# DeltaNet heads: turning the triangular inverses on VectorE, and one run of weight products per level

## The reference

```
# per head, direction and chunk of 64 tokens (the kernel takes blocks of 128)
L = jnp.where(strict, jnp.einsum('bhncd,bhnjd->bhncj', kb, k) * decay, 0.0)
A = L + jnp.eye(C, dtype=L.dtype)
rhs = jnp.concatenate([vb, kb * jnp.exp(gc)[..., None]], axis=-1)
sol = lax.linalg.triangular_solve(A, rhs, left_side=True, lower=True, unit_diagonal=True)
u, w = sol[..., :dv], sol[..., dv:]
...
s = jnp.einsum('bhgqd,bhkd->bhgqk', q_blk, k) * scale
p = jax.nn.softmax(s, axis=-1)
o = jnp.einsum('bhgqk,bhkd->bhgqd', p, v)
```

## Time and profile before

| | us |
|---|---|
| median of 3 runs | 2656.44 (2653.32 to 2656.96) |
| profiled execution, its own time | 2658.15 |
| its span, first to last instruction | 2656.5 |
| TensorE busy | 2560.8, 96% |
| VectorE busy | 1425.2, 54% |
| ScalarE busy | 1022.2, 38% |
| GpSimd busy | 214.3, 8% |
| turns of T (L1669), busy, 448 instructions | 58.0 |
| mean granted clock of TensorE | 0.983 |

### The profile page before, as it was taken

How to read it: one execution, slowest core, us unless ns; L and a number is a source line. 1 busy time by engine, 2 the same in 40 slices (tenths; PEclk the granted TensorE clock), 3 DMA queues, 4 the chain that set the end, 5 groups by cost and what they waited for, 6 DMA issues and landing times.

```text
span 2656.5 us, 35703 instructions
## 1 busy us (share of the span) xinstructions
PE 2560.8 (96%) x12302; PEld 2098.3 (79%) x12302; DVE 1425.2 (54%) x1854; ACT 1022.2 (38%) x1428; POOL 214.3 (8%) x286
## 2 busy tenths in 40 slices
PE   4999999999999899979999999999999999999997
PEld 4777788888887688857888888888888888888885
DVE  6736666666666655464444444444444444444454
ACT  4335435434434343334443234442344432222334
POOL 3401121121121112000000000000000000000000
PEclk7999999999999999999999999999999999999998
DMA  9933454454443535323333333333333323333333
GB/s 349 317 107 111 127 154 116 133 148 120 144 140 113 151 104 155 106 63 95 95 96 91 98 103 95 95 89 98 105 95 97 100 84 98 103 95 95 89 92 127
DMA packets 431664, 318.21 MB, mean 120 GB/s; under 512 B 12886, under 2 KB 403841, under 8 KB 431105
## 3 DMA queue, kind: packets, MB, share of 16 engines
q1 hardware_dynamic: 401648, 212.19, 27.8%
q0 software_dynamic: 29184, 104.87, 12.4%
q10 hardware_dynamic: 785, 0.51, 0.1%
HBM read 313.33 MB, written 4.19 MB: 120 GB/s over the span
## 4 chain that ended last, share of the span: by engine, by line
PE 92%; DVE 3%; DMA 1%; issue 1%; ACT 1%; POOL 0%; DVEq 0%; ACTq 0%; POOLq 0%
PE pw L1399 23%; PE pw L1401 23%; PE pw L1400 23%; PE pw L1383 2%; PE pw L1384 2%; PE pw L1385 2%; PE pd L1669 2%; PE pd L1692 2%; PE pd L1705 2%; PE pd L1652 1%; PE pd L1712 1%; DMA ka<-in_w_ada_dram 1%; DMA T<-in_w_ada_dram 1%; PE pd L1728 1%; PE pd L1723 1%
## 5 line engine op out<-in xcount | busy, mean ns | idle before, releaser
L1399 PE MATMUL pw<-act_hi,w_hi 128*128 128x512 f32 x2016 | 812.7, 403 | 13.9 <-DVE act_lo L1294 8.7
L929 DVE TENSOR_TENSOR w_lo<-raw,w_hi 128x1024 fp32r<-128x1024 f32 x426 | 520.7, 1222 | 519.2 <-ACT w_hi L555 516.7
L1401 PE MATMUL pw<-act_hi,w_lo 128*128 128x512 f32 x2016 | 787.3, 391 | 0.0
L1400 PE MATMUL pw<-act_lo,w_hi 128*128 128x512 f32 x2016 | 785.6, 390 | 0.0
L555 ACT ACTIVATE w_hi<-raw 128x1024 fp32r<-128x1024 f32 x426 | 450.1, 1057 | 503.3 <-PE pw L1401 408.6
L1399 PEld LDWEIGHTS pw<-act_hi,w_hi 128*128 128x128 f32 x2016 | 379.3, 188 | 106.6 <-issue 23.8
L1401 PEld LDWEIGHTS pw<-act_hi,w_lo 128*128 128x128 f32 x2016 | 378.9, 188 | 81.4
L1400 PEld LDWEIGHTS pw<-act_lo,w_hi 128*128 128x128 f32 x2016 | 379.7, 188 | 80.3 <-issue 6.9
L1399 PE MATMUL pw<-mh_hi,w_hi 128*128 128x512 f32 x704 | 276.0, 392 | 1.6 <-DVE w_lo L929 1.6
L1401 PE MATMUL pw<-mh_hi,w_lo 128*128 128x512 f32 x704 | 274.2, 389 | 0.0
L1400 PE MATMUL pw<-mh_lo,w_hi 128*128 128x512 f32 x704 | 274.0, 389 | 0.0
(11 more groups left out here) (278 smaller groups left out, 2639.2 us busy)
## 6 DMA issues: line engine op xcount, KB each, us to landing
raw<-in_w_up_dram SPq DMA_DIRECT2D x176, 512.0 KB, 4.0
ada_w<-in_w_ada_dram POOLq DMA_DIRECT2D x128, 512.0 KB, 4.4
raw<-in_w_in_dram SPq DMA_DIRECT2D x84, 512.0 KB, 3.9
raw<-in_w_down_dram SPq DMA_DIRECT2D x64, 384.0 KB, 3.4
raw<-in_w_down_dram SPq DMA_DIRECT2D x64, 320.0 KB, 3.1
raw<-in_w_out_dram SPq DMA_DIRECT2D x32, 512.0 KB, 4.4
DD<-in_w_ada_dram POOLq DMA_DIRECT2D x9, 512.0 KB, 8.1
EG<-in_w_ada_dram POOLq DMA_DIRECT2D x9, 512.0 KB, 7.0
```

Of the source, the lines that this page charges most:

```text
L929: V.tensor_tensor(w_lo[slot][:], raw[slot][:], w_hi[slot][:].bitcast(F32), ALU.subtract).then_inc(lo_made.sem, 1)
L1399: M(bank, w_hi[slot][:, k, :], hi[:, k0 + k, :], start=first, stop=False)
L1400: M(bank, w_hi[slot][:, k, :], lo[:, k0 + k, :], start=False, stop=False)
L1401: ins = M(bank, w_lo[slot][:, k, :], hi[:, k0 + k, :], start=False, stop=last)
```

## The change

VectorE turns the used 32x32 or smaller blocks of the inverses; its transpose turns each 32x32 block in place, which suffices for levels 0 to 5, whose blocks are up to 32 wide. For level 6 (blocks of 64) VectorE gathers the used columns of both T into `XT`, TensorE turns four blocks of it, and ScalarE copies the bank back. The two T swap places in their buffer (`T_of`), so that the used columns of both are one access pattern. The turns of level 0's `LTm` go to VectorE too, and L1178 reads `XT` in place of the bank. On TensorE, each level has one run of stream steps, behind the XT products. Between a level's two products lie: scores(2) at level 1; turn(0) and scores(3) at 2; turn(1) and the turns of k at 3; turn(2) and those of v at 4; turn(3) at 5; the product of the attention with v at 6. ScalarE's copies of k and v move behind weigh(3) and turned(2). GpSimd's mask for level 1 waits for VectorE's turn in place of TensorE's.

```diff
+        T_of = [T[:, 1], T[:, 0]]
+        def used_columns(n):
+            flat, w = two(T[:]), 1 << n
+            return bass.AP(flat.tensor, flat.offset, [flat.ap[0], [2 * w, S // (2 * w)], [S + w, 2], [1, w]])
...
@@ gpsimd
                     elif n == 1:
-                        pool.wait_ge(*lt_sum.after(h))
+                        pool.wait_ge(*lt_turned.after(h))
@@ scalar
-                for i, (to, bank) in enumerate(((ktf, pd[2]), (vtf, pd[0]))):
+                def by_token(i):
                     act.wait_ge(*tr_sum.after(h, i + 1))
-                    nc.scalar.activation(to, bank, ACT.Copy).then_inc(tok_done.sem, 1)
+                    nc.scalar.activation((ktf, vtf)[i], pd[2 + i], ACT.Copy).then_inc(tok_done.sem, 1)
...
                 def level(n):
-                    for d in range(2):
-                        act.wait_ge(*x_sum.after(h, 2 * (n - 1) + d + 1))
-                        q = 1 - d
-                        nc.scalar.activation(alternate(XTf, 1 << n)[:, :, q], alternate(pd[2 + d], 1 << n)[:, :, q], ACT.Copy) \
-                            .then_inc(xt_taken.sem, 1)
+                    if n == LEVELS - 1:
+                        act.wait_ge(*x_sum.after(h, 1))
+                        nc.scalar.activation(XTf, pd[2], ACT.Copy).then_inc(xt_taken.sem, 1)
...
                 weigh(3)
+                by_token(0)
                 level(4)
                 s(6)
                 turned(2)
+                by_token(1)
                 evacuate_next(2)
@@ vector
+                def turned(n):
+                    V.transpose(XTf, used_columns(n)).then_inc(xt_made.sem, 1)
+                def gathered():
+                    V.tensor_copy(alternate(XTf, 1 << LEVELS - 1), used_columns(LEVELS - 1)).then_inc(xt_made.sem, 1)
...
                     if n < LEVELS - 1:
                         dve.wait_ge(*t_added.after(h, 2 * n))
+                        if n == LEVELS - 2:
+                            gathered()
                         compact(n + 1)
+                    if n < LEVELS - 2:
+                        turned(n + 1)
                 score_max(0)
                 ada_next(1)
-                dve.wait_ge(*lt_sum.after(h))
+                dve.wait_ge(*lm_made.after(h, 1))
+                dve.wait_ge(*rope_step.after(h))
+                V.transpose(XTf, one(LTm)).then_inc(lt_turned.sem, 1)
+                dve.wait_ge(*lt_turned.after(h))
                 eye = ident.unsqueeze(1).broadcast_to([P, NB, P])
                 for d in range(2):
-                    V.scalar_tensor_tensor(T[:, d], blocks(pd[5]), cst[:, C_PAR + d:C_PAR + d + 1], eye, ALU.mult, ALU.add) \
+                    V.scalar_tensor_tensor(T_of[d], XT[:], cst[:, C_PAR + d:C_PAR + d + 1], eye, ALU.mult, ALU.add) \
                         .then_inc(t_first.sem, 1)
                 dve.wait_ge(*t_first.after(h))
                 compact(1)
+                turned(1)
                 score_max(1)
@@ tensor
-                for bank, t in ((pd[2], k_f), (pd[0], v_f)):
+                run(20, 24)
+                def by_token(i):
+                    if i:
+                        pe.wait_ge(*dq_made.after(h))
                     for b in range(NB):
-                        ins = TR(blk(bank, b), blk(t, b), ident)
+                        ins = TR(blk(pd[2 + i], b), blk((k_f, v_f)[i], b), ident)
                     ins.then_inc(tr_sum.sem, 1)
-                run(20, 24)
...
                 scores(1)
-                pe.wait_ge(*lm_made.after(h, 1))
-                for b in range(NB):
-                    ins = TR(blk(pd[5], b), LTm[:, b, :], ident)
-                ins.then_inc(lt_sum.sem, 1)
                 run(24, 28)
-                stops = ((28, 31, 34), (34, 37, 40), (40, 43, 46), (46, 49, 52), (52, 55, 57), (57, 60, 62))
+                stops = (28, 34, 40, 46, 52, 57, 62)
                 for n in range(1, LEVELS):
-                    if n == 1:
-                        pe.wait_ge(*t_first.after(h))
-                        pe.wait_ge(*tok_done.after(h, 1))
-                        pe.wait_ge(*dq_made.after(h))
-                    else:
-                        pe.wait_ge(*t_added.after(h, 2 * (n - 1)))
-                    inverse_turned()
+                    if n == LEVELS - 1:
+                        pe.wait_ge(*tok_done.after(h, 1))
+                        pe.wait_ge(*xt_made.after(h, n))
+                        used_turned()
                     pe.wait_ge(*lm_made.after(h, n + 1))
                     pe.wait_ge(*w_made.after(h, n))
...
-                    run(stops[n - 1][0], stops[n - 1][1])
-                    pe.wait_ge(*xt_taken.after(h, 2 * n))
+                    if n == LEVELS - 1:
+                        pe.wait_ge(*xt_taken.after(h))
+                    else:
+                        pe.wait_ge(*xt_made.after(h, n))
                     pe.wait_ge(*z_taken.after(h, n))
                     for b in range(NB):
                         ins = M(ab[:, b * (P // 2):(b + 1) * (P // 2)], XT[:, b, :], Zc[:, b, :], start=True, stop=True)
                     ins.then_inc(a_sum.sem, 1)
-                    run(stops[n - 1][1], stops[n - 1][2])
+                    run(stops[n - 1], stops[n])
```

More of the change, by code:

```diff
@@ L186, in build @@
         CT, LTm = CL[:, 0], CL[:, 1]
+        T_of = [T[:, 1], T[:, 0]]
+        Tf = [one(t) for t in T_of]
+        def used_columns(n):
+            flat, w = two(T[:]), 1 << n
+            return bass.AP(flat.tensor, flat.offset, [flat.ap[0], [2 * w, S // (2 * w)], [S + w, 2], [1, w]])
         TT, kg = PTb[:, 0:2], PTb[:, 2:4]
@@ L337, in build @@
         pt_taken = signal("pt_taken", NB)
-        xt_taken = signal("xt_taken", 2 * (LEVELS - 1))
+        xt_taken = signal("xt_taken")
         z_taken = signal("z_taken", LEVELS - 1)
@@ L353, in build @@
         av_sum = signal("av_sum")
-        lt_sum = signal("lt_sum")
-        x_sum = signal("x_sum", 2 * LEVELS)
+        lt_turned = signal("lt_turned")
+        xt_made = signal("xt_made", LEVELS - 1)
+        x_sum = signal("x_sum", 3)
         z_sum = signal("z_sum", LEVELS - 1)
@@ L781, in head @@
                 s(7)
-                for d in range(2):
-                    act.wait_ge(*x_sum.after(h, 2 * (LEVELS - 1) + d + 1))
+                act.wait_ge(*x_sum.after(h))
                 act.wait_ge(*av_sum.after(h))
@@ L1152, in score_norm @@
                     V.tensor_scalar(prob[b % 2], prob[b % 2], soft[:, 3, b:b + 1], None, ALU.mult).then_inc(soft_step.sem, 1)
-                Tf = [one(T[:, d]) for d in range(2)]
+                def turned(n):
+                    V.transpose(XTf, used_columns(n)).then_inc(xt_made.sem, 1)
+                def gathered():
+                    V.tensor_copy(alternate(XTf, 1 << LEVELS - 1), used_columns(LEVELS - 1)).then_inc(xt_made.sem, 1)
                 def compact(n):
@@ L1658, in turn @@
                         pe.wait_ge(*pt_taken.after(h, b))
-                    else:
-                        pe.wait_ge(*tok_done.after(h, 2))
                     for k in range(NB):
@@ L1663, in turn, with used_turned @@
                     ins.then_inc(pt_sum.sem, 1)
+                def used_turned():
+                    for b in range(NB):
+                        ins = TR(blk(pd[2], b), XT[:, b, :], ident)
+                    ins.then_inc(x_sum.sem, 1)
                 def inverse_turned():
@@ L1668, in inverse_turned @@
                         for b in range(NB):
-                            ins = TR(blk(pd[2 + d], b), T[:, d, b, :], ident)
+                            ins = TR(blk(pd[2 + d], b), T_of[d][:, b, :], ident)
                         ins.then_inc(x_sum.sem, 1)
@@ L1700, in head @@
                         turn(n - 2)
-                    run(stops[n - 1][0], stops[n - 1][1])
-                    pe.wait_ge(*xt_taken.after(h, 2 * n))
-                    pe.wait_ge(*z_taken.after(h, n))
-                    for b in range(NB):
-                        ins = M(ab[:, b * (P // 2):(b + 1) * (P // 2)], XT[:, b, :], Zc[:, b, :], start=True, stop=True)
-                    ins.then_inc(a_sum.sem, 1)
-                    run(stops[n - 1][1], stops[n - 1][2])
-                    if n == 5:
+                        if n < 5:
+                            by_token(n - 3)
+                    else:
                         pe.wait_ge(*pt_taken.after(h))
@@ L1713, in head @@
                         ins.then_inc(av_sum.sem, 1)
+                    if n == LEVELS - 1:
+                        pe.wait_ge(*xt_taken.after(h))
+                    else:
+                        pe.wait_ge(*xt_made.after(h, n))
+                    pe.wait_ge(*z_taken.after(h, n))
+                    for b in range(NB):
+                        ins = M(ab[:, b * (P // 2):(b + 1) * (P // 2)], XT[:, b, :], Zc[:, b, :], start=True, stop=True)
+                    ins.then_inc(a_sum.sem, 1)
+                    run(stops[n - 1], stops[n])
                 pe.wait_ge(*t_added.after(h))
```

(2 more changed lines are left out.)

## The result

The changed kernel takes 2663.38 us, median of 10 runs (2657.89 to 2665.34); the kernel before took 2656.63 beside it (10 runs, 2653.32 to 2657.74). The ratio is 1.0022, 95% interval 1.0014 to 1.0030. The change was forecast at 2641.5 in a range of 2630 to 2656: it is slower by 0.2%, and outside the range. The profiled execution took 2662.58 us, its span is 2660.9 (before: 2656.5).

The account below looks back on a forecast made before the run. TensorE, busy for 96% of the span, was taken to bound the kernel. 5.6 - 2.7 - 0.75 - 0.3 = 1.85 us a head, 15 us for eight, took the 2656.44 median to 2641.5, range 2630 to 2656.

Parts of the forecast that it names:

- TensorE's gain: Turns taken off TensorE in each head, plus six saved returns to the stream: 5.6 us a head.
- The six returns: On TensorE, joining each level's two stream runs saves six returns to the stream at 0.06: 0.35 us a head.
- The mask's turns: Four turns of the level mask at level 1, taken off TensorE: 0.44 us a head.
- VectorE's price: Each new transpose on VectorE takes 0.69 us.
- The wait at level 1: TensorE waits 2.7 us a head before level 1's Z, as GpSimd's mask and VectorE's three instructions exclude each other.
- Rival 1: At level 1, no mutual exclusion of VectorE and GpSimd: Z waits only 1.7 us; 2633.5 us in all; chance 0.24.
- The XT wait at level 1: TensorE waits 0.75 us a head before level 1's XT products, for ScalarE's copy of Z.
- Rival 2: TensorE's clock falls to half behind level 1's wait, 1.6 us each; 2654 us if in every head; chance 0.19.
- Rivals 3 and 4: VectorE's transposes much dearer, 2692 us, chance 0.07; TensorE's removed turns hidden anyway, 2656, chance 0.05 including small slips.
- What was expected to cost nothing: Levels 2 to 4 and 6, VectorE's full levels, GpSimd's masks and w_lo for the stream: no TensorE waits.
- The 0.3 of level 5: At level 5 only one softmax turn covers Z's copy, so TensorE waits 0.3 us a head.
- the forecast's own range of 2636 to 2650: Times allowed for the whole kernel under the main forecast of 2641.5 us, without the rivals; chance 0.45.

Follow-up runs that it names:

- e1_fill9: The changed kernel with nine unused stream-sized matmuls on TensorE per head, ahead of level 1's wait: 2651.00 us, 0.9974 of before.
- e2_own_lt: The changed kernel with level 0's mask product in its own buffer, so GpSimd makes level 1's mask without waiting for VectorE's transpose: 2656.19 us, 0.9996 of before.
- e3_run31: The changed kernel with three more stream steps ahead of level 1, taken from behind levels 1 to 3: 2643.58 us, 0.9948 of before.
- e7_max_first: e3_run31 with VectorE's score_max(1) moved ahead of turned(1): 2642.13 us, 0.9946 of before.
- e8_own_lt_30: The changed kernel with e11_own_lt_rope's buffer and mask order, score_max(1) ahead of turned(1), stream stops 30, 35, 41, 46, 52, 57, 62: 2634.63 us, 0.9916 of before.
- e6_wait_before: The kernel before with only a bare wait added on TensorE ahead of level 1's turns in each head: 2692.61 us, 1.0136 of before.
- e5_fill4: The changed kernel with four unused matmuls on TensorE per head, ahead of level 1's wait: 2653.90 us, 0.9993 of before.
- e11_own_lt_rope: e2_own_lt with GpSimd's mask product 1 made after the rotary step: 2652.88 us, 0.9988 of before.

## Why the prediction was wrong, point by point

**TensorE's gain, 5.6 us a head: too large by 0.7.** At full clock (e1_fill9) the period is 1.1 us shorter than before, 1.12 in the head shown. In front of that stand the losses, in this head and from group start to group start: 2.58 for fill and wait at level 1; 0.88 from level 1's weight products to level 2's first group, which takes 7.66 us against 6.78 with the same products and six steps in both; 0.36 at level 5, where it is 0.72 from the softmax turn to the XT products against 0.36 to the stream. Sum 3.82, so the gross gain is 4.94, by difference. Three terms gave less than forecast. The six returns, 0.35: level 2 became 0.91 us shorter, 0.88 of that its turns, and at level 3 stream and softmax turn together took 4.69 us before and take 4.65 now. The 0.06 of a first matmul behind a small group did not vanish, it moved to the next group's start: a softmax turn takes 0.36 up to a stream matmul and 0.45 up to a small group. The mask's turns, 0.44: from the first scores to level 1 it is 4.68 us against 4.92, so 0.24. And levels 5 and 6 together, 15.30 us against 16.07, gave 0.77 after their loss, where the turns alone (1.32 less 0.36) would give 0.96.

**VectorE's price: right.** The transposes of T take 0.70 us each (40 of them), those of the mask too (8); forecast 0.69.

**The wait at level 1: right, and for the reason given.** 19.7 us in eight, 2.37 to 2.53 each, forecast 2.7. Rival 1 (1.7 without exclusion) falls with e2_own_lt: with the mask out of the way the wait is 1.5, so the exclusion is there. What the forecast left open, whether VectorE can be the one that waits, is answered: it is. The rows of VectorE from 220 to 900 us (kernel after: count, busy us, mean ns, idle us):

```profile
L1174 DVE TENSOR_TENSOR Wc<-T 128x256 f32<-128x256 f32 x42 | 36.2, 863 | 1.2
...
L1161 DVE TENSOR_SCALAR tmp<-tmp,soft 128x512 f32<-128x512 f32 x28 | 19.0, 678 | 1.0
...
L1200 DVE SCALAR_TENSOR_TENSOR T<-XT,cst_sb 128x512 f32<-128x512 f32 x14 | 16.5, 1217 | 0.2
L1169 DVE COPY XT<-T 128x512 f32<-128x512 f32 x7 | 11.6, 1650 | 0.2
```

The same three that existed before, in the kernel before:

```profile
L1159 DVE TENSOR_TENSOR Wc<-T 128x256 f32<-128x256 f32 x42 | 17.8, 424 | 1.4
L1152 DVE TENSOR_SCALAR tmp<-tmp,soft 128x512 f32<-128x512 f32 x28 | 13.6, 487 | 1.0
L1178 DVE SCALAR_TENSOR_TENSOR T<-pd,cst_sb 128x512 f32<-128x512 f32 x14 | 9.8, 744 | 0.0
```

Compact doubled, from 424 to 863 ns, and level 5's gathered copy takes 1650 ns where I had counted 0.5 us. In the shorter levels GpSimd's mask starts within 0.5 us of the compact for levels 3 to 5 and of the gathered copy; before, compact never met it. In the changed kernel it was harmless, since levels 2 to 4 keep their cover (no wait there), but compact and the copy are what TensorE waits for at levels 5 and 6 in e3_run31, e7_max_first and e8_own_lt_30. That the masks beside them cause this lateness is read from the traces, no run isolates it. The Trainium skill (SBUF — State Buffer, section "Who interferes with whom") lists copies and tensor_scalar in certain modes among those that take the shared pair, and says that whoever issues first keeps it for the whole instruction. The rows of this trace agree: the softmax scaling, a tensor_scalar with one tensor input, took 1.42 us beside a mask in this head and 0.49 without one. I had drawn on the half of that rule about two SBUF inputs only.

**The XT wait at level 1: right.** Forecast 0.75; at full clock it is 0.55 of idle time and 0.88 from start to start. With the 2.58 ahead of it level 1 costs 3.46 us, and 2.7 + 0.75 were forecast; two small misses cancel. e7_max_first confirmed the chain that the forecast named (score_max, weigh, Z's copy).

**The clock: the step that failed.** The sum has no term for it: behind the waits of 2.7 and 0.75 it lets TensorE go on at full clock. Rival 2 is what happens, in eight heads of eight, and it had a chance of 0.19. I had two rows to go by the earlier trace rows, a wait of 2.98 us that kept the clock and one of 1.87 that lost it, and took the forecast that ignored the clock as the likelier. e1_fill9 and e6_wait_before show it as cause, on either kernel. Its price was given as 1.6 us a head, 13 in all; e1_fill9 stands 12.4 us below the changed kernel. That the total fits is luck, since it is made up otherwise: 1.0 us where 3.4 us are spent at half clock, 2.7 where 6.8 are. The longer kind was not in the forecast.

**The sum redone.** Full clock: 4.94 - 2.58 - 0.88 - 0.36 = 1.12 us a head, 9 us of span for eight (2656.5 to 2647.5), against 15 forecast. Clock: the span of the changed kernel is 13.4 us longer than that of e1_fill9. By the prices above, seven heads up to the last one's first mask (four at 2.7, three at 1.0) give 13.8 us, and the traces show 13.5 there. The last head fell for 6.8 us too, but from its first mask to the end of the kernel only 0.7 us were lost; the stretch ahead of the first head was 0.8 shorter. So the loss by the clock turns a gain of 9 us into a span 4.4 us longer. Without it the kernel comes out near 2650 (e1_fill9 by its ratio to before), at the slow end of the forecast's own range of 2636 to 2650. Rival 2 as priced (2654) missed because it stood on 15 us of gain, not 9. Rivals 3 and 4 do not occur.

**What was expected to cost nothing** held: no w_lo late for the stream, no waits at levels 2 to 4, 0.3 us twice at level 6. The 0.3 of level 5 is 0.36 from start to start, without showing as idle. But VectorE's levels had little room: with three steps fewer at levels 1 to 3 (e3_run31) TensorE waits for it at levels 5 and 6.

## What to carry over

A wait on the engine that sets the time is not priced by its length alone: ask what runs behind it, and whether the clock comes back at once. Here 2.4 us of idle time in each head cost the kernel before 4.3 us a head, and useless matmuls in place of such waits saved the changed kernel 12 us. Moving an operation from a full engine to one with room pays only if the work that covers it moves along: the same change with two more stream steps ahead of the first level, the mask out of the way, and the maximum first and one more ahead of the last was 1.0% faster than before instead of 0.2% slower. And when a phase gets shorter, look again at which instructions of VectorE and GpSimd now meet.

## What the runs showed of the hardware

Whether the granted clock falls after an idle time is not set by its length alone. At 1.5 to 1.7 us it fell in 2, 5 or 6 of 8 heads (e5_fill4, e11_own_lt_rope, e2_own_lt), and the stretch that followed was 3.4 or 6.8 us long. In one execution of e11_own_lt_rope, with the same instructions in each head, heads 0 to 2 kept the clock behind 1.49 to 1.57 us and heads 3 to 7 lost it behind 1.49 to 1.56. Even the wait of 2.98 us at the start of the heads, which kept the clock in the kernel before, is followed by a low one in e11_own_lt_rope (windows and timeline of TensorE):

```profile
205.00:209.00 4.00, 4.00 (x13) 0.65 0.39 112
```

```profile
203.40 0.47 PE L1422 MATMUL pw<-act_hi,w_hi 128*128 128x512 f32 x1 [2.98 <-DVE w_lo L938]
```

So a row that kept the clock once proves little. What else decides stays open. The Trainium skill (TensorE: Matmul & The Clock Gate, "HAM oscillation") warns of a clock that falls again at each repeated gap; the falls in all eight heads at 2.4 to 2.5 us agree, and at 1.5 to 1.7 us the clock fell at some of the repeated gaps and not at others.

Not tried: keeping GpSimd's masks away from compact by issuing its loads behind the mask instead of ahead of it. That the loads set the meeting is read from the trace of the kernel after, not shown by a run.
